# A fifth seven-product block pair in each column pair of a squared-ReLU MLP

## The reference, cut to what matters

```
h2 = rmsnorm(x, norm2_g[l])
x  = x + jnp.square(jax.nn.relu(h2 @ w_up[l])) @ w_down[l]     # w_up 2048 x 8192, w_down 8192 x 2048
```

## Time and profile before

| | |
|---|---|
| median of 3 runs | 2036.02 us (2035.47 to 2036.15) |
| profiled execution | 2035.84 us, of which the span is 2034.0 us |
| busy share of the span | PE 100%, weight loads (PEld) 84%, DVE 73%, ACT 59%, POOL 11% |
| TensorE clock | full (1.00) |

### The profile page before, as it was taken

One profiled execution on the slowest core, in us unless ns is written; L12 is line 12 of the kernel. 1 busy time (PEld: TensorE's weight loads), 2 busy tenths in 40 slices (PEclk: granted clock), 3 DMA queues, 4 the chain that ended last, 5 costly groups with the idle time before them and its releaser, 6 DMA issues.

```text
span 2034.0 us, 27169 instructions
## 1 busy us (share of the span) xinstructions
PE 2028.2 (100%) x10602; PEld 1702.3 (84%) x10602; DVE 1482.5 (73%) x1917; ACT 1190.1 (59%) x1572; POOL 225.7 (11%) x228
## 2 busy tenths in 40 slices
PE   9999999999999999999999999999999999999999
PEld 7887788888888888888888877888888888888887
DVE  7767556688679668868777775666886796697685
ACT  6557644566466457556545576445655664575563
POOL 6254100000000000002023531000000000000000
PEclk9999999999999999999999999999999999999999
DMA  9477966677667676767654678666776786777674
GB/s 302 130 230 191 233 183 185 185 216 230 188 197 241 196 201 211 225 187 202 205 175 144 218 199 225 188 184 188 227 216 187 201 241 194 202 215 220 189 212 130
DMA packets 182815, 411.35 MB, mean 202 GB/s; under 512 B 14122, under 2 KB 22800, under 8 KB 182688
## 3 DMA queue, kind: packets, MB, share of 16 engines
q1 hardware_dynamic: 173968, 379.52, 61.1%
q0 software_dynamic: 8544, 30.01, 8.3%
q10 hardware_dynamic: 176, 0.09, 0.0%
HBM read 377.95 MB, written 2.12 MB: 187 GB/s over the span
## 4 chain that ended last, share of the span: by engine, by line
PE 99%; DVE 0%; issue 0%; ACT 0%; DVEq 0%
PE psum L636 23%; PE psum L612 21%; PE psum L639 12%; PE psum L616 10%; PE psum L679 10%; PE psum L682 5%; PE psum L646 3%; PE psum L647 3%; PE psum L650 3%; PE psum L729 2%; PE psum L730 2%; PE psum L733 2%; PE psum L744 1%; PE psum L818 1%; PE psum L797 0%; PE psum L843 0%
## 5 line engine op out<-in xcount | busy, mean ns | idle before, releaser
L941 ACT CAST w_hi<-raw_ring 128x1024 fp32r<-128x1024 f32 (+1 forms) x720 | 743.7, 1041 | 711.3 <-PE psum L639 319.6
L1182 DVE TENSOR_TENSOR w_lo<-raw_ring,w_hi 128x1024 fp32r<-128x1024 f32 (+1 forms) x664 | 811.6, 1230 | 422.0 <-ACT w_hi L941 420.2
L636 PE MATMUL psum<-xt,w_hi 128*128 128x512 f32 x2048 | 513.3, 392 | 0.3 <-issue 0.3
L636 PEld LDWEIGHTS psum<-xt,w_hi 128*128 128x128 f32 x2048 | 368.7, 189 | 67.0 <-issue 0.7
L639 PEld LDWEIGHTS psum<-xt,w_lo 128*128 128x128 f32 x2048 | 279.4, 190 | 20.0
L639 PE MATMUL psum<-xt,w_lo 128*128 128x256 f32 x2048 | 285.6, 282 | 0.0
L612 PE MATMUL psum<-w_hi,xt 128*128 128x512 f32 (+1 forms) x1152 | 281.5, 386 | 0.3 <-ACT w_hi L941 0.3
L612 PEld LDWEIGHTS psum<-w_hi,xt 128*128 128x128 f32 x1152 | 202.4, 188 | 41.2 <-issue 2.7
L679 PE MATMUL psum<-w_hi,ht_lo 128*128 128x512 f32 x448 | 174.4, 389 | 0.0
L679 PE MATMUL psum<-w_hi,ht_hi 128*128 128x512 f32 x448 | 174.4, 389 | 0.0
L1738 POOL DMA_DIRECT2D lo_own<-raw_ring x28 | 24.2, 865 | 1184.7 <-ACT lo_own L957 1184.7
(11 more groups left out here) (210 smaller groups left out, 2451.8 us busy)
## 6 DMA issues: line engine op xcount, KB each, us to landing
raw_ring<-in_w_up_dram SPq DMA_DIRECT2D x256, 512.0 KB, 3.9
raw_ring<-in_w_down_dram SPq DMA_DIRECT2D x256, 512.0 KB, 4.7
raw_ring<-in_w_in_dram SPq DMA_DIRECT2D x128, 512.0 KB, 4.7
raw_ring<-in_w_out_dram SPq DMA_DIRECT2D x64, 512.0 KB, 4.9
w_lo<-raw_ring POOLq DMA_DIRECT2D x28, 512.0 KB, 6.3
lo_own<-raw_ring POOLq DMA_DIRECT2D x28, 512.0 KB, 5.9
raw_ring<-in_w_in_dram SPq DMA_DIRECT2D x16, 256.0 KB, 2.9
x<-in_x_dram SPq DMA_DIRECT2D x8, 256.0 KB, 7.3
```

Source lines behind the costliest of these rows:

```text
L636: pe.matmul(bank[:, f, :], w_hi[:, w, j, f * P:(f + 1) * P], both, start=kt == 0, stop=False, skip_group_check=True)
L941: act.copy(w_hi[:, u % AHEAD, :, 0:cols], raw_ring[:, u % RAWS, :, 0:cols]).then_inc(hi_ready, 1)
L1182: dve.tensor_tensor(w_lo[:, u % AHEAD, :, 0:cols], raw_ring[:, u % RAWS, :, 0:cols], w_hi[:, u % AHEAD, :, 0:cols].bitcast(F32), ALU.subtr ...
```

## The change

Each stage now has five seven-product pairs, at the places p1, p3, p4, p6 and p7 (`SEVEN_AT`). The pairs are taken in another order (`ORDER`): the blocks of the old pairs 4 and 5 change places, and pair 6 (`EXTRA`), formerly plain, becomes the fifth. Two seven-product pairs now follow directly on another one: p4 on p3, and p7 on p6. For such a follower (`follows_seven`) ACT makes `t_hi` two units later than for the others, ahead of the `w_hi` of the second unit after the pair, and DVE makes its `t_lo` likewise. The first sums of a follower are made at the end of the step of the pair before. The token sums of the extra pair are made in d = 0 by themselves, once a turn: four small DVE operations into `s_raw` at step w5, `extra_hi` on ACT at w6, `extra_lo` on DVE at w7.

The units whose low part comes by DMA are now w0 and w10 of a stage (they were w0 and w8), and ACT negates them five steps ahead instead of six. The first seven-product pair of d = 0 now does its second unit first as well, and the wait for a freed bank moves from its start to its middle. In the last pair the product with `t_lo` that frees the fourth bank is no longer done ahead of the others. POOL's start on the next layer's tables waits for `extra_done` instead of `s_done`. The weights are loaded in the new order; the number and size of the loads do not change.

```
 SEVEN = (1, 3, 5, 7)
+EXTRA = 6
+ORDER = [(0, 1, 2, 3, 5, 4, EXTRA, 7)] * 2
+SEVEN_AT = [(1, 3, 4, 6, 7)] * 2
-SUMMED_PAIR = [LOOP0 + LOOP_UNITS * i + 16 * d + m for i in range(LOOPS) for d in range(2) for m in (0, 8)]
+SUMMED_PAIR = [LOOP0 + LOOP_UNITS * i + m for i in range(LOOPS) for m in (0, 10, 16, 26)]
-NEGATED_AHEAD = 6
+NEGATED_AHEAD = 5
...
+        def follows_seven(pl, u):
+            return seven_at(pl, u) is not None and seven_at(pl, u - 2) is not None
...
# PE, seven_products
-                if first and d == 0:
-                    pe.wait_ge(evicted[0], pl.evictions(18))
-                swap = last or first and d == 1
+                if kp == EXTRA:
+                    pe.wait_ge(extra_done, pl.l * TURNS + pl.i + 1)
+                swap = last or first
...
# ACT, split_hi
                 act.wait_ge(unit_done, pl.unit(u + 1))
+                if follows_seven(pl, u - 2) and seven_at(pl, u - 2)[0] == 1:
+                    t_hi_of(seven_at(pl, u - 2)[1])
...
-                if seven is not None and seven[0] == 1:
-                    act.wait_ge(t_raw_ready, seven[1] + 1)
-                    if seven[1]:
-                        act.wait_ge(sevens_done, seven[1])
-                    act.copy(t_hi[:, :, :], t_raw[:, :, :]).then_inc(t_hi_ready, 1)
+                if seven is not None and seven[0] == 1 and not follows_seven(pl, u):
+                    t_hi_of(seven[1])
...
# ACT, activations
+                if part == "pair" and c == 0 and k == 6:
+                    act.wait_ge(extra_raw, pl.l * TURNS + pl.i + 1)
+                    act.copy(extra_hi[:, :, :], s_raw[:, 0, :, :]).then_inc(extra_cast, 1)
...
# DVE, split_lo
+                if follows_seven(pl, u - 2) and seven_at(pl, u - 2)[0] == 1:
+                    t_lo_of(seven_at(pl, u - 2)[1])
...
+                if seven is not None and seven[0] == 1:
+                    if pair_at(pl, u)[1:] == (1, 2 * SEVEN_AT[1][0] + 1):
+                        take_totals(pl, pair_at(pl, u)[0])
+                    if not follows_seven(pl, u):
+                        t_lo_of(seven[1])
+                    if after is not None:
+                        first_sums(pl, u + 1)
...
# DVE, mlp
+                if part == "pair" and c == 0 and k == 5:
+                    dve.wait_ge(s_done, pl.l * 2 * TURNS + 2 * pl.i + 2)
+                    sums_of(slice(EXTRA % 4, EXTRA % 4 + 1), 1, extra_raw)
+                if part == "pair" and c == 0 and k == 7:
+                    dve.wait_ge(extra_cast, pl.l * TURNS + pl.i + 1)
+                    dve.tensor_tensor(extra_lo[:, :, :], s_raw[:, 0, :, :], extra_hi[:, :, :].bitcast(F32), ALU.subtract).then_inc(extra_done, 1)
```

More of the change, by code:

```diff
@@ L202, in encoder @@
         w_lo = sb("w_lo", [P, AHEAD, 2, CW], F32R)
+        with ExitStack() as extra:
+            extra_hi, extra_lo = [extra.enter_context(nc.sbuf_tensor(f"extra_{h}", [P, 4, P], F32R)) for h in ("hi", "lo")]
         head_in = sb("head_in", [P, RT * CW])
@@ L664, in pair_steps @@
             def pair_steps(pl, s, d, m):
-                kp, half = m // 2, m % 2
+                kp, half = ORDER[d][m // 2], m % 2
                 a, b = k_blocks(kp)
@@ L685, in seven_products @@
             def seven_products(pl, s, d, kp, a, b):
-                i, first, last = SEVEN.index(kp), kp == SEVEN[0], kp == KPS - 1
+                first, last = kp == SEVEN[0], kp == KPS - 1
                 _, number = seven_at(pl, s)
@@ L690, in seven_products @@
                     pe.wait_ge(s_done, pl.l * 2 * TURNS + 2 * pl.i + kp // 4 + 1)
-                if first and d == 0:
-                    pe.wait_ge(evicted[0], pl.evictions(18))
-                swap = last or first and d == 1
+                if kp == EXTRA:
+                    pe.wait_ge(extra_done, pl.l * TURNS + pl.i + 1)
+                swap = last or first
                 def s_tile(n):
-                    return [t[:, i, n, :] for t in (s_hi, s_lo)]
+                    if kp == EXTRA:
+                        return [t[:, n, :] for t in (extra_hi, extra_lo)]
+                    return [t[:, SEVEN.index(kp), n, :] for t in (s_hi, s_lo)]
                 def own():
+                    if first and d == 0:
+                        pe.wait_ge(evicted[0], pl.evictions(18))
                     if first and d == 1:
@@ L723, in seven_products @@
                 pe.wait_ge(t_hi_ready, number + 1)
[L724 to L727, removed]
                 for bank, (a_hi, a_lo), t, start in products:
@@ L731, in seven_products @@
                 pe.wait_ge(t_lo_ready, number + 1)
-                for bank, (a_hi, a_lo), t, start in products:
+                for n, (bank, (a_hi, a_lo), t, start) in enumerate(products):
                     mm = pe.matmul(bank, a_hi, t_lo[:, t, :], start=False, stop=True, skip_group_check=True)
+                    if last and n == 0:
+                        mm.then_inc(pair_done, 1)
                 mm.then_inc(sevens_done, 1)
@@ L1173, in split_lo @@
             def split_lo(pl, u, cols=CW):
-                after = seven_at(pl, u + 1)
-                if after is not None and after[0] == 0:
+                if follows_seven(pl, u - 2) and seven_at(pl, u - 2)[0] == 1:
+                    t_lo_of(seven_at(pl, u - 2)[1])
+                after, seven = seven_at(pl, u + 1), seven_at(pl, u)
+                if after is not None and after[0] == 0 and seven is None:
                     first_sums(pl, u + 1)
-                seven = seven_at(pl, u)
                 if seven is not None and seven[0] == 0:
@@ L1187, in split_lo, with t_lo_of @@
                                       ALU.subtract).then_inc(t2_ready, 1)
[L1188 to L1192, removed]
+            def t_lo_of(number):
+                dve.wait_ge(t_hi_ready, number + 1)
+                dve.tensor_tensor(t_lo[:, :, :], t_raw[:, :, :], t_hi[:, :, :].bitcast(F32), ALU.subtract).then_inc(t_lo_ready, 1)
             def first_sums(pl, u):
@@ L1716, in _ @@
                 if l:
-                    pool.wait_ge(s_done, l * 2 * TURNS)
+                    pool.wait_ge(extra_done, l * TURNS)
                 rope_tables(l)
```

30 lines of the change are left out of this document (18 added, 12 removed).

## The result

| | before | changed |
|---|---|---|
| time, median | 2036.09 us (2035.47 to 2037.14, 4 runs) | 2110.32 us (2109.12 to 2111.34, 4 runs) |
| span of the profiled execution | 2034.0 us | 2108.2 us |
| mean granted clock | 1.000 | 0.994 |

The ratio is 1.0364, 95% interval 1.0352 to 1.0376: slower by 74 us, where 66 were predicted (2102, range 2047 to 2120).

A forecast was written before the change was run, and what follows sets the result against it. PE was taken to bound the kernel, with DVE nearly a second bound in d = 0. Six turns of 6.15 + 2.95 us (54.6) plus 2 x 5.55 (11.1) gave 65.7 more, 2102 us, range 2047 to 2120.

The forecast's parts named there:

- Only d = 0 and d = 1 grow: Pair stages carry the loss, 6.15 and 2.95 us longer in full turns; the up stage costs nothing more.
- p4 of d = 0: `s_lo` comes 2.7 us late at its head, then `t_hi` late behind `extra_hi`: 4.7 us lost.
- p7 of d = 0: PE waits for `w_hi` and `w_lo` of the second unit, now first; stage ends 6.15 us longer in all.
- Bank copies: Start of d = 1: p7's `t_hi` pushes the copies back, the eighth ends late, 0.8 us lost.
- The DMA into `lo_own`: For w16 it lands at 468.0, needed at 469.6; for w10 also in time: not late.
- d = 1: Banks 0.8, p4 1.35, last unit's `w_lo` 1.5, less 0.68 saved: stage 2.95 us longer than 41.00.
- The two last stages: Last turn of each layer, where no negation follows: 5.55 us longer each, 11.1 together.
- The sum: Whole kernel: 54.6 us from six full turns plus 11.1 from the last stages, 65.7 longer, so 2102.
- second case: PE's restart after each halt takes 0.25 instead of 0.05 to 0.1 us: 16 us more, 2118.
- Rival A: Whole kernel faster: DVE's lead of four units absorbs the added work and PE's work decides; 2023.7 us, chance 6%.
- Rival B: Pair stages: only DVE's throughput counts and its waits for ACT close up; 2049 us, chance 12%.
- Rival D: Halts at p4 drop TensorE's clock to 1.2 GHz, 5 us more in each of eight d = 0 stages; 2142, 9%.

The follow-up runs named there:

- Experiment 4: Changed kernel with five seven-product pairs only in d = 1; d = 0 back to four in the old order, swap kept: 2047.24 us, ratio 1.0055.
- experiment 5: Kernel before, with only the second unit first in p1 of d = 0 and the bank wait moved to its middle: 2032.84 us, ratio 0.9985.
- experiment 9: Changed kernel with half of the `w_lo` columns in pair stages, `extra_hi` one unit later and the negation one unit earlier: 2035.10 us, ratio 0.9997.
- experiment 6: Changed kernel with `extra_hi` one unit later on ACT, behind `t_hi`, and the negation one unit earlier: 2083.47 us, ratio 1.0234.
- Experiments 8: Changed kernel with `w_lo` made for half the columns in the pair stages, sums not the reference's: 2053.27 us, ratio 1.0088.
- experiment 2: Changed kernel with DVE making `s_lo` before the first sums of p4 instead of behind `w_lo` of w8: 2114.67 us, ratio 1.0385.
- experiment 1: Changed kernel with `extra_hi` one unit later on ACT, behind the `t_hi` of p4: 2092.63 us, ratio 1.0278.
- experiment 7: Changed kernel with `extra_hi` later, the negation earlier, and POOL instead of DVE making each seven-product pair's two weight differences: 2149.04 us, ratio 1.0560.

## Why the prediction was right, and by how much it was off

- **Only d = 0 and d = 1 grow.** Right: the up stages kept their length, and 61.2 + 13.1 us in the pair stages are everything. Experiment 4 splits it: a fifth pair in d = 1 alone costs 14.4 us over experiment 5 (2.4 a turn), the one in d = 0 brings the rest.
- **p4 of d = 0.** Right in each link: `s_lo` is there at 443.72 (443.5), the extra sums end at 445.90 (445.7), `t_hi` at 447.93 (447.8), DVE rests 2.06 (2.2). p4 loses 5.03 us in the third turn, 4.7 predicted. The 0.3 is mostly the restarts after its three halts (0.08, 0.11 and 0.11).
- **p7 of d = 0.** Right in its links; 2.68 us lost in the third turn, 2.45 worked out (7.15 over 40.15, less the 4.7). In the first turn the matmul waited until 462.66 (462.1) and the clock took more.
- **Bank copies.** 0.8 predicted in each full turn. In the last four full turns they cost 0.57 at one start, about 1.0 with the smaller delays and restarts around it; in the first two nothing, where the slower clock lets p7 end later.
- **The DMA into `lo_own`.** Said not to be late. Its median landing went from 5.9 to 7.6 us, and in one turn, the third, PE waited 0.81 for it. The step failed there, but it costs nothing in the whole: p4 loses as much less behind it, and the stage takes 44.12 us like the others.
- **d = 1.** Right term by term in the fourth to sixth turns: p4 lost 1.3 (1.35), p7 1.65 (1.5), the beginning 1.0 (0.8). The stage took 44.12 us; the 43.95 looks closer than it was, since it starts from 41.00 where 40.83 is right. The increase was 3.29, predicted 2.95.
- **The two last stages.** 5.55 longer predicted, 6.90 and 6.20 measured. The longer one is the first layer's, and there the prediction put POOL's tables for the next layer at nothing. They run beside DVE from 998.77 on, the last third of this stage, and three `w_lo` ahead of p7 took 3.86 us where they took 3.49 in the other; PE got `w_lo` 0.78 us later after the stage's start. That POOL is the reason is read from this pair of stages and from POOL's own times below, 1.30 us beside DVE and 0.32 while DVE rests; no run moves the tables.

```profile
1006.56 3.86 DVE L1201 TENSOR_TENSOR w_lo<-raw_ring,w_hi 128x1024 fp32r<-128x1024 f32 x3
2054.46 3.49 DVE L1201 TENSOR_TENSOR w_lo<-raw_ring,w_hi 128x1024 fp32r<-128x1024 f32 x3
```

```profile
1006.78 1.30 POOL L1708 TENSOR_TENSOR rope_c<-const,gains 128x64 f32<-128x64 f32 x1
...
1013.91 0.32 POOL L1708 TENSOR_TENSOR rope_c<-const,gains 128x64 f32<-128x64 f32 x1
```

- **The sum.** 65.7 predicted, 74.3 measured. At full clock d = 0 became 6.75 us longer instead of 6.15, six times 3.6 us; d = 1 3.29 instead of 2.95, six times 2.0; the first two turns are 0.5 longer each than the others, for the clock, 1.0; the two last stages make 2.0. That is the 8.6. The mis-sized term of d = 0 is what PE loses around its halts: the prediction took 0.05 to 0.1 for hand-overs and left out the second start after a halt, 0.30 to 0.34 instead of 0.2267, which makes 0.48 of the 0.6. In d = 1 there are such restarts too; their part of the 0.34 was not taken apart. The prediction's second case, 0.25 for each hand-over, was summed too high: six turns of eight halts and two stages of four are 56 halts, and 0.15 to 0.2 more for each is 8 to 11 us, not 16.
- **Rival A** (PE's work decides) fell: even with half of `w_lo` left out, experiment 9 is at 2035.1. The prediction says that the stretches before bear out a change of the bounding engine; they do not, since PE is the busiest in all three of the earlier trace rows. In the changed kernel it is DVE in d = 0 (41.95 against 41.59 in the third turn). **Rival B** (throughput alone, 2049) fell too: experiment 6, which takes away the two places where ACT's order holds DVE up, comes nearest to its premise and is 34 us above it.
- **Rival D** (the clock) came true in part. The changed kernel by stretches, p4 and p7 of the first turn, columns as above:

```profile
442.00:444.00 2.00, 0.19 (x1) 0.22 (x2) 2.00 (x3) 2.00 (x3) 0.86 (x1) 1.00 0.29 29
444.00:446.00 2.00, 2.00 (x6) 1.57 (x6) 1.84 (x5) 0.06 (x1) 0.00 (x0) 0.57 0.82 197
446.00:448.00 2.00, 2.00 (x6) 1.55 (x6) 0.03 (x1) 2.00 (x3) 0.00 (x0) 0.58 1.05 238
462.00:464.00 2.00, 0.88 (x3) 0.47 (x4) 1.27 (x2) 2.00 (x3) 0.72 (x1) 1.00 0.35 53
464.00:466.00 2.00, 2.00 (x7) 1.56 (x8) 1.13 (x1) 2.00 (x3) 0.00 (x0) 0.69 0.99 266
466.00:468.00 2.00, 2.00 (x7) 1.52 (x6) 1.87 (x4) 1.94 (x5) 0.00 (x0) 0.50 1.05 221
```

The clock goes to its lower level, 1.2 GHz, behind the rests, and 6 or 7 matmuls fit where 9 did. The Trainium skill, TensorE: Matmul & The Clock Gate, Part 1, has a halved clock come back with idleness, and these rows agree, though not every such rest lowers it (last section). The price was not 5 us a stage: in p4 the slow matmuls fill time in which PE would wait for `t_hi` anyway (the 1.17 at 811.79 comes at full clock and is missing in the first turn). In p7 of the first two turns there is nothing behind which to hide; in the first d = 0 takes 49.54 instead of 47.92, and 1.1 of these 1.6 us come back in d = 1 (43.04 instead of 44.12).

What remains open: whether five pairs can win. Experiments 8 and 9 say that this needs room on DVE, though not how much, and the waits of 9 that it needs an earlier place for the bank copies as well; no version that computes everything was found below the kernel before except experiment 5, which leaves the pairs alone.

## What to carry to other kernels

Before work is moved from the busiest engine to the next one, add up the next one's work stage by stage: here DVE was busy 73% of the whole but 92% of the stage that got most of the new work, and a lead of four units did not carry the excess across. Then follow each new operation through every in-order stream that it enters, since two engines that wait for each other's results pass their lateness on (DVE's rest of 2.06 us came from its own sums by way of ACT), and price each halt with its restart. The longest wait of the bounding engine need not be worth anything: 23 us at `s_lo` were worth 4 or less, while a single line of order on another engine was worth 17.7.

## What the runs showed of the hardware that was not expected

- TensorE's clock fell without any long rest. In experiment 2 it fell behind halts of 1.25 and 0.64 us, while in experiment 1 a rest through the same 2 us left it at full speed. In the changed kernel the same halt of 2.9 us was followed by the lower level in the first two turns and not in the third (clock 0.93, 0.93 and 1.00 over d = 0). Experiments 2 and 1 by stretches, 2 first:

```profile
442.00:444.00 2.00, 1.29 (x3) 0.80 (x4) 1.51 (x3) 2.00 (x3) 0.82 (x1) 0.84 0.00 0
444.00:446.00 2.00, 2.00 (x6) 1.61 (x5) 1.93 (x5) 0.77 (x1) 0.04 (x1) 0.50 0.73 121
```

```profile
442.00:444.00 2.00, 0.00 (x0) 0.00 (x0) 2.00 (x3) 2.00 (x3) 0.86 (x1) 1.00 0.00 0
444.00:446.00 2.00, 1.45 (x6) 1.23 (x7) 1.97 (x4) 2.00 (x2) 0.00 (x0) 1.00 0.72 133
```

  What decides it between the two was not found.
- The first start after a halt lies 0.30 to 0.34 us ahead of the next one, against 0.2267 in a running stream (827.63, 827.97, 828.20 above).
- VectorE and GpSimd operations on SBUF were slower side by side: 2.28 instead of 1.22 us and 2.13 instead of 1.27 us for one operation (experiment 7). In the first layer's last stage a `w_lo` beside POOL's tables took about 0.12 us longer (three in 3.86 against 3.49 us), and a table operation 1.30 instead of 0.32 us.
